# Pre-adding the squared outputs on VectorE in the retention heads of a hybrid decoder kernel

## The reference, cut to what matters

```
def rms_norm(x, g=None):
    xf = x.astype(jnp.float32)
    y = xf * lax.rsqrt(jnp.mean(xf * xf, axis=-1, keepdims=True) + EPS)
...
def retention_out(o, gate, w_out):
    B, T = o.shape[:2]
    o = rms_norm(o).reshape(B, T, RET_HEADS * RET_DV).astype(gate.dtype)
    return (jax.nn.silu(gate) * o) @ w_out
```

## Time and profile before

| | |
|---|---|
| time, median of 3 runs | 2298.31 us (2297.2 to 2301.33) |
| span of the profiled execution, first to last instruction | 2295.4 us |
| TensorE busy | 2099.1 us, 91% of the span |
| VectorE busy | 887.8 us, 39% |
| ScalarE busy | 621.2 us, 27% |
| GpSimd busy | 581.0 us, 25% |

### The profile page before, as it was taken

How to read it: one execution, slowest core, us unless ns; L and a number is a source line. 1 busy time by engine, 2 the same in 40 slices (tenths; PEclk the granted TensorE clock), 3 DMA queues, 4 the chain that set the end, 5 groups by cost and what they waited for, 6 DMA issues and landing times.

```text
span 2295.4 us, 37322 instructions
## 1 busy us (share of the span) xinstructions
PE 2099.1 (91%) x16087; PEld 1932.8 (84%) x16087; DVE 887.8 (39%) x989; ACT 621.2 (27%) x725; POOL 581.0 (25%) x132
## 2 busy tenths in 40 slices
PE   5989999999979999999796997988787889999998
PEld 5969879888869999999796995665555789999998
DVE  4344352453465142435442234552222354334241
ACT  4222322322242111112322134443333131111121
POOL 2303404214033333333232231000000123333331
PEclk8999999999989999999998998999999899999999
DMA  4341342332422222221324110005887312222221
GB/s 145 111 156 38 111 165 65 129 120 92 147 83 74 74 89 75 73 91 56 100 73 140 57 55 10 1 1 207 326 326 299 102 56 77 89 73 88 77 73 59
DMA packets 168640, 240.01 MB, mean 105 GB/s; under 512 B 12898, under 2 KB 131810, under 8 KB 168210
## 3 DMA queue, kind: packets, MB, share of 16 engines
q1 hardware_dynamic: 156738, 214.11, 27.7%
q10 hardware_dynamic: 11712, 23.76, 2.8%
q0 software_dynamic: 80, 0.52, 0.1%
HBM read 212.26 MB, written 26.12 MB: 104 GB/s over the span
## 4 chain that ended last, share of the span: by engine, by line
issue 51%; PE 31%; POOL 9%; ACT 3%; DVE 2%; DMA 2%; SPq 1%; POOLq 0%; ACTq 0%
POOL w_lo L660 9%; PE PS L705 7%; PE PS L704 7%; PE PS L706 7%; PE PS L1028 2%; DMA k_page<-in_cache_k 2%; PE PS L1003 1%; PE PS L1064 1%; PE PS L1026 1%; PE PS L1082 1%; ACT k_page_t L1453 1%; PE PS L1075 1%; PE PS L1114 1%; PE PS L1011 1%; ACT probs_t L1432 1%
## 5 line engine op out<-in xcount | busy, mean ns | idle before, releaser
L660 POOL TENSOR_TENSOR w_lo<-w_raw,w_hi 128x2048 fp32r<-128x2048 f32 x125 | 578.0, 4624 | 1671.9 <-ACT w_hi L1188 1671.9
L704 PE MATMUL PS<-x_hi,w_hi 128*128 128x296 f32 x1792 | 540.5, 302 | 24.0 <-DVE x_lo L1526 18.2
L1188 ACT ACTIVATE w_hi<-w_raw 128x2048 fp32r<-128x2048 f32 x125 | 239.6, 1917 | 1129.3 <-PE PS L706 893.9
L705 PE MATMUL PS<-x_lo,w_hi 128*128 128x296 f32 x1792 | 541.0, 302 | 0.0
L706 PE MATMUL PS<-x_hi,w_lo 128*128 128x296 f32 x1792 | 538.7, 301 | 0.0
L704 PEld LDWEIGHTS PS<-x_hi,w_hi 128*128 128x128 f32 x1792 | 341.7, 191 | 27.7 <-issue 23.2
L705 PEld LDWEIGHTS PS<-x_lo,w_hi 128*128 128x128 f32 x1792 | 341.4, 190 | 0.3 <-issue 0.2
L706 PEld LDWEIGHTS PS<-x_hi,w_lo 128*128 128x128 f32 x1792 | 341.1, 190 | 0.0
L705 PE MATMUL PS<-hidden_lo,w_hi 128*128 128x296 f32 x1024 | 307.2, 300 | 0.0
L706 PE MATMUL PS<-hidden_hi,w_lo 128*128 128x296 f32 x1024 | 306.1, 299 | 0.0
L704 PE MATMUL PS<-hidden_hi,w_hi 128*128 128x296 f32 x1024 | 305.8, 299 | 0.0
(11 more groups left out here) (205 smaller groups left out, 2470.8 us busy)
## 6 DMA issues: line engine op xcount, KB each, us to landing
w_raw<-in_w_mlp_up SPq DMA_DIRECT2D x32, 1024.0 KB, 5.3
w_raw<-in_w_mlp_down SPq DMA_DIRECT2D x32, 1024.0 KB, 5.0
k_page<-in_cache_k SPq DMA_DIRECT2D x64, 512.0 KB, 6.1
v_page<-in_cache_v SPq DMA_DIRECT2D x64, 512.0 KB, 6.5
w_raw<-in_w_ret_in SPq DMA_DIRECT2D x24, 1024.0 KB, 5.3
sample_state<-in_state_ret SPq DMA_DIRECT2D x32, 512.0 KB, 5.4
out_state_ret_sample<-sample_state ACTq DMA_DIRECT2D x32, 512.0 KB, 4.3
w_raw<-in_w_ret_out SPq DMA_DIRECT2D x16, 512.0 KB, 3.4
```

The lines of the kernel that those rows point to most:

```text
L660: pool.tensor_tensor(WL[n.slot][:], WR[n.slot][:], WH[n.slot][:].bitcast(F32), ALU.subtract) \
L704: pe.matmul(o, wh[:, w], xh[:, t, cols], start=(t == 0), stop=False)
L705: pe.matmul(o, wh[:, w], xl[:, t, cols], start=False, stop=False)
L1188: act.activation(WH[n.slot][:], WR[n.slot][:], ACT.Copy).then_inc(hi_done, 1)
```

## The change

For each half of the tokens VectorE first adds value tiles 0 and 1 to tiles 2 and 3 in one instruction (128x592), then the two results in another (128x296), in place in `TT4`. TensorE waits for the new semaphore `osq_sum` instead of `osq_done` and multiplies ones by one tile instead of four. In VectorE's program the first pair of adds stands after the last update of the prompt's state and ahead of `new_state` 4; the second pair stands behind `new_state` 7.

```
             def sum_squares(hf, h):
-                pe.wait_ge(osq_done, 2 * h + 2 - hf)
+                pe.wait_ge(osq_sum, 2 * h + 2 - hf)
                 pe.wait_ge(o_evac, 5 * h + 4)
-                for v in range(4):
-                    last = pe.matmul(PS[:, 4 + hf, 0:HF], ck("ones"), TT4[:, v, :], start=(v == 0), stop=(v == 3))
-                last.then_inc(osq_used, 1)
+                pe.matmul(PS[:, 4 + hf, 0:HF], ck("ones"), TT4[:, 0, :], start=True, stop=True).then_inc(osq_used, 1)
...
+                def add_tiles(hf):
+                    dve.wait_ge(osq_done, 2 * h + 2 - hf)
+                    do(dve.tensor_tensor(TT4[:, 0:2, :], TT4[:, 0:2, :], TT4[:, 2:4, :], ALU.add))
+                    dve.tensor_tensor(TT4[:, 0, :], TT4[:, 0, :], TT4[:, 1, :], ALU.add).then_inc(osq_sum, 1)
+
+                add_tiles(1)
                 for b in range(4, DB):
                     new_state(b, 0 if b % 2 == 0 else 6)
+                add_tiles(0)
...
-            PER_HEAD = 13
+            PER_HEAD = 15
```

More of the change, by code:

```diff
@@ L407, in program @@
         osq_used = sem("osq_used")
+        osq_sum = sem("osq_sum")
         oroot_done = sem("oroot_done")
```

## The result

The changed kernel takes 2339.76 us in the median of 4 runs (2331.14 to 2348.12); the kernel before, run beside it, takes 2299.82 us (2297.2 to 2302.48). The ratio is 1.0176, with a 95% interval of 1.0145 to 1.0206: 40 us slower. The forecast was 2314 us, slower too, but the result lies outside its range of 2300 to 2325.

The account below looks back on a forecast made before the run. TensorE, busy 91% of the span, was taken as the bound, with head-end delays counting in full. Waits of +2.3 us and lost clock of 13.7 us gave +16.0 on the median 2298.31: 2314 us, range 2300 to 2325.

Parts of the forecast that it names:

- the kind of loss in the heads: Each head's second sum waits for VectorE behind `new_state` 7, some 3 us idle; +2.3 us together at full clock.
- The 0.47 us expected in the fourth head: Gain from the fourth head's first call, where TensorE was to start L787 without waiting for the sample states' transfer.
- the clock: Idle TensorE at each head's end falls to 1.2 GHz: 13.7 us over four heads, bounds 6.8 and 27.
- Rival A: Every head waits for VectorE and loses the clock: 2307 to 2328 us, likeliest 2314; chance 0.70.
- one fall like the third head's: Low stretch at a head's end, 7.0 us at granted clock 0.51: 3.4 us of full clock lost per head.
- B: Heads lose only the wait for VectorE, the clock falls no more often than before: 2300.6 to 2301.6 us; chance 0.14.
- the step that says what moves: Placed the whole loss at the heads' ends, +16.0 us, and expected none in the units or the MLP.
- theory P: From the experiments, not the prediction: a TensorE loop touching eight 256-instruction packets has lost its first when it branches back.
- E: Clock stays low longer, over L787 and through the unit in every head: above 2328 us; chance 0.08.
- D: VectorE's adds run long by meeting a GpSimd weight split: +22 us for four heads, 2336 us; chance 0.02.

Follow-up runs that it names:

- the padding: Changed kernel with 48 wait instructions on TensorE ahead of the first MLP, so later code stands where it stood before: 2318.34 us, ratio 1.0097 to the kernel before.
- the early adds: Changed kernel with 48 wait instructions and the second pair of adds moved behind `new_state` 5: 2303.12 us, ratio 1.0036 to the kernel before.

## Why the prediction was right and wrong

**Right: the kind of loss in the heads.** The second sum waits for VectorE behind `new_state` 7, 2.56 to 2.84 us of idle time where some 3 were forecast; the adds take 0.77 and 0.47 us where 0.775 and 0.46 stood in the sum. By the Trainium skill, "VectorE: DVE Perf Modes", section on the TRN2 errata, the second would be an estimate of 466 ns; the 468 ns measured agree. In the first head the first call gained nothing, since the transfer's wait follows. The 0.47 us expected in the fourth head are not to be seen: TensorE waited for the sample states there (its L788 starts at 612.67 us, 3.5 us after the sum began).

**Right within its bounds: the clock.** Rival A's sum gave +16.0 us with bounds on the clock of 6.8 to 27; with the code back in its place the span grew by 17.0 and the median by 19.4. The single terms were less good. They assume one fall like the third head's in every head; the end of the fourth ran at 1.2 GHz for 17.1 us, and of the 16.8 us by which its unit came late with the padding the head itself added 10.0, and the first only 1.2. The total came out right because the errors had both signs. The 1 us between 17.0 and the forecast is luck besides, since single traces of these heads differ by more. That the low clock is what costs there on balance is supported by the stretches of 0.50 in the heads, 51.2 us with the padding against 13.7 before: 37.5 us more at half speed are worth at most 18.8 us, while the waits of 14.3 us over eight calls stand against 11.9 us of saved passes. It is not shown by itself, since no run changes the clock and nothing else. B, the wait alone, would have ended at 2301.6.

**Wrong: the step that says what moves.** The prediction says that "a loss in the units or in the MLP" is where "I expect none"; the sum has no term for the length of TensorE's program. The work of the MLP did not change, but its code did: 48 instructions fewer ahead of it moved the last MLP's loop to a place from which every pass fetches its code again; by theory P its body lay in seven packets of 256 instructions and now lies in eight. Then each pass fetches its instructions anew, with two pauses and a stretch of half clock, 7 us a pass, 21 us in three. That is the missing 20 us: the forecast, which leaves it out, is 2314, and 2318.3 were measured with the code in its old place. No rival had it: E put a longer low clock into the heads, and D, adds that run long, did not occur.

Was it to be foreseen? The seven-or-eight count needs the body's length and its place within a packet. The length can be counted; with 22 or 23 bad places of 256 (by theory P), a change of place has about 9 chances in 100 to hit one. The place itself could have been read from the packet times of the kernel before. By the Trainium skill, "Runtime: NRT & Kernel Launch", "Instruction fetch mechanics", TensorE's instruction memory holds 2048 instructions in blocks of 256, is refilled in order, and a taken branch to a target outside the current window of two blocks waits for its fetch. The runs agree with the block of 256 and with the wait, not with the window of two: a loop of seven blocks is branched back in within 0.2 us and without a fetch. 2048 instructions are eight blocks, and by theory P a loop of eight is not kept. Why not is only argued: the packet behind the loop, the ninth of each pass, is fetched as well.

## What to carry to other kernels

Removing instructions is not local: it moves all code behind it on that engine. Where a hardware loop of over a thousand instructions follows, count the packets that its body touches, and compare the instruction queue's packets of two profiles before explaining anything else; a few waiting instructions ahead of the loop take the effect out of a comparison.

When work is handed to an engine with time to spare, its place in that engine's queue counts more than its length: 1.2 us of adds behind the wrong update cost some 13 us over four heads, of which 9.6 are waits and the rest agrees with the clock that the waiting engine lost. Filling the idle time with unused matmuls took the early adds from 1.0036 to 1.0012, no better than the kernel before, and gained nothing in that kernel itself (1.0009).

## What the runs showed of the hardware

A loop on TensorE of 1559 or of 1655 instructions is branched back in within 0.2 us and fetches nothing from most places (104.95 us a pass); from others each branch back takes 4.7 to 5.1 us, nine packets of instructions are fetched and a pass is 4.4 to 7.7 us longer. Seven packets against eight is the count that fits all these runs. A loop of some 2150 instructions, that over heads 0 to 2, fetched again in every run, with 3.3 to 3.9 us a branch. A waiting instruction whose semaphore is long set cost nothing that shows when 96 were spread over a pass of matmuls (104.96 us), and 16.1 us for 170 in a row, 95 ns each, with nothing to cover them.

A low stretch of the clock in the heads lasted from 3.4 to 17.1 us in these runs; the longest covered all of a head's last small products, up to 3 us into the unbroken matmuls of the unit (second head of the changed kernel: unit from 328.7, stretch to 331.5).
